# Sharing the expert sums of the context tokens among ScalarE, Pool and VectorE, and moving their end into the output merge

## The chip, the cores and the metric

The kernel runs on 1 core of one Trainium2 chip. The metric is device time in microseconds (us) of one execution. PE is the matrix engine, DVE VectorE, ACT ScalarE, POOL or Pool GpSimd, and SP the queue that issues most loads.

## The reference, cut to what matters

Two layers work on 512 latent tokens and, with a learned modulation of their own, on 128 context tokens. Each token mixes (attention, short convolution, bidirectional recurrence, merged by gates), is normalised, and then passes through a layer of experts: for each token 8 heads x 16 best keys choose 128 experts, each with a row u and a row v of 1024 numbers.

```
        ue = jnp.take(u_tab, idx, axis=0)
        ve = jnp.take(v_tab, idx, axis=0)
        act = jax.nn.gelu(jnp.einsum('td,thkd->thk', xb, ue).astype(jnp.float32), approximate=False)
        return jnp.einsum('thk,thkd->td', (g * act).astype(ve.dtype), ve)
...
    ff = peer(h, p['peer_wq'], p['peer_keys'], p['peer_u'], p['peer_v'])
    x = layer_norm(DEEPNORM_ALPHA * x + g_f * ff, p['ln_g'][1], p['ln_b'][1])
```

For the 128 context tokens, one per partition, this means 128 dot products of `h` with a gathered row u and 128 weighted sums `y += w * v`. The modulated result is the next layer's input (`h_ctx`), and the last layer's is the output `y_prompt`.

## The kernel before

A layer runs as a row of stages; all engines meet between two of them. In the order of the program: input and mixing of the context tokens (`context_in`), a scan, `context_out`, then for the latent tokens `recurrent_branch` (projection, scan, second projection with the tiles `rf_`, second scan), `recurrent_out` (`recm`), `conv_branch` (`conv_`), `attention` (projection `qkv_`, then `attention_core`, tiles `att_`), `attention_out` (the output merge, tiles `attm_`), `context_end` (tiles `ce_`), and `experts` for the latent tokens (about half of the time).

All projections are one function, `projections` (L161). A job multiplies the tokens with a 1024 x 1024 weight matrix in two halves. SP loads a matrix of 2 MB into `ring` (two buffers); ACT rounds each half to a high part, and DVE forms the low part by a subtraction (`low_part`, L152, the "split"); PE needs both. PE then fills output tiles, which ACT or DVE empties. After tile t DVE may run a number of small jobs of another party, the object `behind`: `hooks` (L178) spreads its `n_vector` jobs evenly over the tiles. Pool runs the party's `pool` or `pool_all`.

That party is the experts of the context tokens (`ContextExperts`, L2202). Pool gathers a row of u or v for all 128 tokens with one indirect DMA of 512 KB (L2307) into one of five slots of `ctx_rows`; a gather waits until the slot's last user is done. DVE makes a dot product in one instruction (L2313) or adds `w * row` to `ctx_y` in one (L2337). `DOTS = 24, 56, 48` gives the dots in the stages `rf_`, `recm` and `conv_`; `SUMS = 48, 52, 28` the sums in `conv_`, `qkv_` and `attm_`, all of them on DVE. In `rf_`, Pool also refines the gates of the recurrence (L1051, L1052, 16 pairs), and gathers stand between the pairs. Dots in `conv_` use three slots and sums two; before and after that sums use five.

In the attention core DVE works through 32 units (a head of a block of 128 tokens: a maximum L873, a difference of two softmaxes L882, a division L887), and Pool has nothing. In layer 0 that stage also computes the next layer's modulation from 12 weight loads of 2 MB (L402). In the merge, Pool works on vectors for the next part (L1128 to L1132).

`context_end` (L2963) loads six rows, forms `LN(alpha x + gate y)`, stores it, and for layer 0 modulates, transposes it on PE and copies it to `h_ctx` on ACT.

## Time and profile before

| | |
|---|---|
| median of 3 runs | 6462.62 us (6458.78 to 6463.95) |
| profiled execution | 6454.55 us, its span 6452.7 us, mean granted clock 0.949 |
| busy: PE | 5330.4 us (83%) |
| busy: DVE | 4310.9 us (67%) |
| busy: ACT | 2317.6 us (36%) |
| busy: POOL | 1969.1 us (31%) |

The span is the time from the first to the last instruction. A busy share is an average over all stages, and says little here: stages differ in what ends last in them. The rows further down are therefore cut by stage. Times in a timeline count from the span's start. "Idle before" is the engine's time without work ahead of an instruction, and behind the arrow stands what ended it. An instruction's duration includes time in which it was held by another engine.

### The profile page before, as it was taken

To read this page: it belongs to the slowest core of one execution; us is meant where nothing else is said; L and a number is where in the kernel's file an instruction comes from. 1 tells how busy PE (TensorE), PEld (TensorE's weight loads), DVE (VectorE), ACT (ScalarE), POOL (GpSimd) and SP (SyncE) were. 2 spreads that over 40 slices of the span, in tenths; PEclk is the share of its full clock that TensorE was granted. 3 is DMA by queue.
4 is the path that set the end of the run, shared out by engine and by line. 5 is a ranking of instruction groups with operands and counts; after the bars stand their busy time and mean duration, and the time that the engine had idled before them with its cause. 6 is when DMAs were issued, how large, how long until landed. Compare 5 with 4: busy or idle time off the path is not lost. (4 is left out here: it accounts for less than half of the span.)

```text
span 6452.7 us, 92227 instructions
## 1 busy us (share of the span) xinstructions
PE 5330.4 (83%) x34024; PEld 3655.2 (57%) x34024; DVE 4310.9 (67%) x8431; ACT 2317.6 (36%) x5243; POOL 1969.1 (31%) x1837
## 2 busy tenths in 40 slices
PE   7979868988868888888789798789889688888886
PEld 6758757777764333333267687677677533333332
DVE  3147767877677777777741377768787777777777
ACT  1122552222414444444412135521233244444444
POOL 0002434442114333333300024344421233333332
PEclk8989989999989999999999899899999899999999
DMA  8732226776449999999976323277743699999998
GB/s 343 311 154 81 89 78 233 281 258 228 180 157 418 421 421 421 420 418 419 416 282 233 154 81 101 77 256 272 251 142 140 231 421 421 421 421 419 415 419 342
DMA packets 296531, 1813.69 MB, mean 281 GB/s; under 512 B 35120, under 2 KB 58864, under 8 KB 141940
## 3 DMA queue, kind: packets, MB, share of 16 engines
q0 software_dynamic: 221184, 1342.28, 52.3%
q1 hardware_dynamic: 74902, 465.54, 18.9%
q8 instruction: 273, 4.47, 0.3%
q14 instruction: 172, 1.41, 0.1%
HBM read 1792.74 MB, written 17.04 MB: 280 GB/s over the span
## 5 line engine op out<-in xcount | busy, mean ns | idle before, releaser
L2093 PE MATMUL ex_ps_y<-ring,peer_small 128*128 128x512 f32 x1632 | 789.4, 611 | 201.2 <-ACT peer_small L2043 199.1
L2093 PE MATMUL ex_ps_y<-early,peer_small 128*128 128x512 f32 x1632 | 785.1, 609 | 203.4 <-ACT peer_small L2043 201.4
L1934 DVE CUSTOM_DVE_ANT_0 early<-early,ex_ps_h 128x1024 f32<-128x1024 f32 x408 | 498.0, 1220 | 299.1 <-DMA early<-in_peer_uv,ex_index 295.6
L1934 DVE CUSTOM_DVE_ANT_0 ring<-ring,ex_ps_h 128x1024 f32<-128x1024 f32 x408 | 497.8, 1220 | 286.3 <-DMA ring<-in_peer_uv,ex_index 282.6
L2035 ACT ACTIVATE ex_act<-ex_dot 128x1 f32<-128x1 f32 x1024 | 205.6, 201 | 1261.1 <-DVE ex_dot L1934 1260.0
L2307 POOL DMA_INDIRECT ctx_rows<-in_peer_uv,ctx_iv x256 | 357.6, 1397 | 921.4 <-DVE ctx_y L2337 541.1
L2093 PEld LDWEIGHTS ex_ps_y<-early,peer_small 128*128 128x128 f32 x1632 | 285.3, 191 | 622.4 <-issue 622.0
L2093 PEld LDWEIGHTS ex_ps_y<-ring,peer_small 128*128 128x128 f32 x1632 | 285.3, 191 | 622.0 <-issue 621.6
L1670 POOL DMA_INDIRECT early<-in_peer_uv,ex_index x408 | 395.1, 968 | 633.6 <-PE ex_ps_y L2093 567.1
L1670 POOL DMA_INDIRECT ring<-in_peer_uv,ex_index x408 | 388.5, 952 | 649.5 <-PE ex_ps_y L2093 593.5
L2093 PE MATMUL ex_ps_y<-ex_slot,peer_small 128*128 128x512 f32 x832 | 407.7, 617 | 114.1 <-ACT peer_small L2043 113.1
L2313 DVE CUSTOM_DVE_ANT_0 ctx_rows<-ctx_rows,ctx_h 128x1024 f32<-128x1024 f32 x256 | 318.3, 1253 | 158.5 <-DMA ctx_rows<-in_peer_uv,ctx_iu 157.9
L2043 ACT ACTIVATE peer_small<-ident,ex_w 128x128 f32<-128x128 f32 x1024 | 411.3, 402 | 33.5
L2307 POOL DMA_INDIRECT ctx_rows<-in_peer_uv,ctx_iu x256 | 329.1, 1286 | 216.3 <-DVE ctx_dots L2313 153.2
L2337 DVE SCALAR_TENSOR_TENSOR ctx_y<-ctx_rows,ctx_dots,ctx_y 128x1024 f32<-128x1024 f32 x254 | 326.9, 1287 | 60.8 <-issue 29.9
L1934 DVE CUSTOM_DVE_ANT_0 ex_slot<-ex_slot,ex_ps_h 128x1024 f32<-128x1024 f32 x208 | 253.7, 1220 | 145.0 <-DMA ex_slot<-in_peer_uv,ex_index 142.9
L1670 POOL DMA_INDIRECT ex_slot<-in_peer_uv,ex_index x208 | 198.7, 955 | 474.8 <-PE ex_ps_y L2093 316.7
L2093 PEld LDWEIGHTS ex_ps_y<-ex_slot,peer_small 128*128 128x128 f32 x832 | 147.5, 194 | 331.2 <-issue 330.9
L2039 ACT ACTIVATE ex_w<-ex_act,ex_share 128x1 f32<-128x1 f32 x1024 | 301.5, 294 | 37.4 <-ACT ex_act L2035 0.4
L2073 PE MATMUL ex_ps_q<-h_high,ex_wh 128*128 128x256 f32 x512 | 236.3, 462 | 26.6 <-DVE h_low L152 26.6
L266 PE MATMUL rf_ps<-rf_wh,h_high 128*128 128x256 f32 x768 | 219.1, 285 | 28.3 <-DVE rf_wl L152 28.3
L266 PE MATMUL conv_ps<-h_high,conv_wh 128*128 128x512 f32 x512 | 210.9, 412 | 27.0 <-DVE conv_wl L152 27.0
(556 smaller groups left out, 12955.2 us busy)
## 6 DMA issues: line engine op xcount, KB each, us to landing
ring<-in_w_in SPq DMA_DIRECT2D x75, 2048.0 KB, 9.1
ci_w<-in_w_in SPq DMA_DIRECT2D x35, 2048.0 KB, 9.8
ring<-in_w_branch SPq DMA_DIRECT2D x23, 2048.0 KB, 10.1
ring<-in_mod_w SPq DMA_DIRECT2D x22, 2048.0 KB, 8.3
room<-in_peer_wq SPq DMA_DIRECT2D x14, 1024.0 KB, 26.1
co_w<-in_w_out SPq DMA_DIRECT2D x4, 2048.0 KB, 14.7
ring<-in_peer_wq SPq DMA_DIRECT2D x4, 2048.0 KB, 13.1
co_w<-in_peer_wq SPq DMA_DIRECT2D x4, 2048.0 KB, 7.9
```

What stands on the lines that cost most here:

```text
L266: last = nc.tensor.matmul(ps[:, at:at + cols], lhs, rhs, start=k == 0 and n == 0, stop=k == KT - 1 and n == 2)
L1670: nc.gpsimd.indirect_dma_start(pair_row[slot(n, s)], None, T["peer_uv"], bass.IndirectOffsetOnAxis(ap=index[n % 4][:, s:s + 1], axis=0)).t ...
L1934: V.tensor_tensor_reduce(out=row, in0=row, in1=ps_h[:], scale=1.0, scalar=0.0, op0=ALU.mult, op1=ALU.add, accum_out=dot[n % 2][:, s:s + 1] ...
L2035: act.activation(act_v[n % 2][:, at], dot[n % 2][:, at], ACT.Gelu).then_inc(gelu_done, 1)
L2039: act.activation(wgt[n % 2][:, at], act_v[n % 2][:, at], ACT.Copy, scale=share[n % 2][:, at]).then_inc(weighed, 1)
L2043: act.activation(diag[s % DIAGS], ident[:], ACT.Copy, scale=wgt[n % 2][:, at]).then_inc(diag_ready, 1)
L2073: last = nc.tensor.matmul(ps_q[:, a, 0:width], w[h % 2][:, k, w_cols], h_split[x][:, k, toks], start=k == 0 and m == 0, stop=k == KT - 1 a ...
L2093: last = nc.tensor.matmul(ps_y[n % 2][:, c:c + 512], diag[s % DIAGS], v_row[slot(n, s)][:, c:c + 512], start=s == 0, stop=s == TOPK - 1)
L2307: self.nc.gpsimd.indirect_dma_start(self.row(s), None, self.table, bass.IndirectOffsetOnAxis(ap=index[:, j:j + 1], axis=0)).then_inc(self. ...
L2313: self.nc.vector.tensor_tensor_reduce(out=self.row(s), in0=self.row(s), in1=self.h[:], scale=1.0, scalar=0.0, op0=ALU.mult, op1=ALU.add, a ...
L2337: V.scalar_tensor_tensor(self.y[:], self.row(s), w, self.y[:], ALU.mult, ALU.add).then_inc(self.added, 1)
```

## The change

The numbers of dots become 6, 58 and 64 in `rf_`, `recm` and `conv_`. The 128 sums are spread in another way:

- `conv_`: 30 sums. ACT scales the gathered row in place by its weight, at a hook of its own after a tile, and Pool adds it to `ctx_y`. The slots are 0 and 1; dots keep slots 2 to 4.
- `qkv_`: 16 sums of the same kind (slots 3 and 4), and 45 on DVE as before (slots 0 to 2), but into `ctx_h`, which is free by then.
- attention core: 20 sums on Pool alone, a scaling and an addition each, with five slots.
- `attm_`: 17 sums on DVE, with slots 0 and 1.

The stage `context_end` goes. `ContextEnd` is the party of the merge: of its 51 hooks on DVE over 36 tiles, the first 17 are the sums (tiles 0 to 11), and hooks 23 to 36 are the steps of the end (tiles 16 to 26); ACT takes the root at a hook. SP loads three rows into slots 2 to 4 ahead of the merge's weights, and the others behind them. The transposes into `h_ctx` are done by the next layer's `context_in`, ahead of its first product.

```
                 beside.load(sp)
+                behind.load(sp)
                 for c, job in enumerate(weighted[1:], 1):
                     if c >= 2:
                         sp.wait_ge(low_done, splits(2 * (c - 2) + 1))
                     sp.dma_start(ring[c % 2][:], job.weights).then_inc(w_loaded[c % 2], 16)
+                behind.load_last(sp)
                 beside.finish(sp)
+                behind.stored(sp)
...
                             act.wait_ge(tile_done, t + 1)
                             empty(act, job, e, t, m, steps).then_inc(slot_free[t % 4], 1)
+                        for j in hooks(behind.n_scalar, t):
+                            behind.scalar(act, j)
...
+            @block.gpsimd
+            def _(pool):
+                behind.pool_all(pool)
...
-DOTS = 24, 56, 48
-SUMS = 48, 52, 28
-U_FIRST, V_FIRST = DOTS[0] + DOTS[1], SUMS[0]
-PHASES = (("u", 0, U_FIRST, (0, 1, 2, 3, 4)), ("u", U_FIRST, CHOICES - U_FIRST, (2, 3, 4)),
-          ("v", 0, V_FIRST, (0, 1)), ("v", V_FIRST, CHOICES - V_FIRST, (0, 1, 2, 3, 4)))
+DOTS = 6, 58, 64
+U_FIRST = DOTS[0] + DOTS[1]
+SUMS = {"conv": 30, "qkv_pool": 16, "qkv": 45, "att": 20, "attm": 17}
+PHASES = (("u", U_FIRST, (0, 1, 2, 3, 4)), ("u", CHOICES - U_FIRST, (2, 3, 4)), ("conv", SUMS["conv"], (0, 1)),
+          ("qkv_pool", SUMS["qkv_pool"], (3, 4)), ("qkv", SUMS["qkv"], (0, 1, 2)), ("att", SUMS["att"], (0, 1, 2, 3, 4)), ("attm", SUMS["attm"], (0, 1)))
+ON_VECTOR = SUMS["qkv"] + SUMS["attm"]
+ON_POOL = CHOICES - ON_VECTOR
...
+    def gather_v(self, pool, phase, j):
+        s, n, behind, v, done = LANDINGS[phase, j]
+        if behind is not None:
+            if phase in ("qkv", "attm"):
+                pool.wait_ge(self.added_too, self.l * ON_VECTOR + behind)
+            else:
+                pool.wait_ge(self.added, self.l * ON_POOL + behind)
+        pool.sem_inc(self.going, 1)
+        self.nc.gpsimd.indirect_dma_start(self.row(s), None, self.table, bass.IndirectOffsetOnAxis(
+            ap=self.index_v[:, v:v + 1], axis=0)).then_inc(self.landed[s], 16)
...
+    def arrived(self, eng, phase, j):
+        s, n, behind, v, done = LANDINGS[phase, j]
+        eng.wait_ge(self.weighed, 2 * self.l + v // 64 + 1)
+        eng.wait_ge(self.landed[s], 16 * (self.l * LANDED[s] + n))
+        return self.row(s), self.dots[:, v:v + 1], done
...
+    def scale(self, eng, phase, j):
+        row, w, done = self.arrived(eng, phase, j)
+        if phase == "att":
+            self.nc.gpsimd.tensor_scalar(row, row, w, None, ALU.mult).then_inc(self.scaled, 1)
+        else:
+            eng.activation(row, row, ACT.Copy, scale=w).then_inc(self.scaled, 1)
+
+    def add_on_pool(self, pool, phase, j):
+        s, n, behind, v, done = LANDINGS[phase, j]
+        P_ = self.nc.gpsimd
+        pool.wait_ge(self.scaled, self.l * ON_POOL + done + 1)
+        if done == 0:
+            P_.tensor_scalar(self.y[:], self.row(s), 1.0, None, ALU.mult).then_inc(self.added, 1)
+            return
+        pool.wait_ge(self.added, self.l * ON_POOL + done)
+        P_.tensor_tensor(self.y[:], self.y[:], self.row(s), ALU.add).then_inc(self.added, 1)
...
-            V.tensor_scalar(self.y[:], self.row(s), w, None, ALU.mult).then_inc(self.added, 1)
+        if done == 0:
...
+        dve.wait_ge(self.added_too, self.l * ON_VECTOR + done)
+        V.scalar_tensor_tensor(self.h[:], row, w, self.h[:], ALU.mult, ALU.add).then_inc(self.added_too, 1)
...
+        e, n, added = self.experts, SUMS["conv"], 0
+        e.gather_v(pool, "conv", 0)
+        e.gather_v(pool, "conv", 1)
         for j in range(DOTS[2]):
-            self.experts.gather(pool, "u", U_FIRST + j)
-            self.experts.gather(pool, "v", j)
...
+            e.gather_u(pool, U_FIRST + j)
+            while added < n and (added + 2) * DOTS[2] <= (j + 1) * n:
+                e.add_on_pool(pool, "conv", added)
+                if added + 2 < n:
+                    e.gather_v(pool, "conv", added + 2)
+                added += 1
+        for j in range(added, n):
+            e.add_on_pool(pool, "conv", j)
+            if j + 2 < n:
+                e.gather_v(pool, "conv", j + 2)
...
+        for j in range(SUMS["qkv"]):
+            e.gather_v(pool, "qkv", j)
+            while added < n and (added + 2) * SUMS["qkv"] <= (j + 1) * n:
+                e.add_on_pool(pool, "qkv_pool", added)
+                if added + 2 < n:
+                    e.gather_v(pool, "qkv_pool", added + 2)
+                added += 1
...
+        e, n = self.experts, SUMS["att"]
+        for j in range(CTX_SLOTS):
+            e.gather_v(pool, "att", j)
+        for j in range(n):
+            e.scale(pool, "att", j)
+            e.add_on_pool(pool, "att", j)
+            if j + CTX_SLOTS < n:
+                e.gather_v(pool, "att", j + CTX_SLOTS)
...
+    n_vector = n_scalar = 3 * SUMS["attm"]
+    FIRST_STEP = SUMS["attm"] + 6
...
+    def load(self, sp):
+        e = self.experts
+        sp.dma_start(self.gate, mod_row(e.T, e.l, 1, 5)).then_inc(self.first_in, 16)
+        sp.dma_start(self.x, e.T["ctx_rows"]).then_inc(self.first_in, 16)
...
+    def load_last(self, sp):
+        e = self.experts
+        sp.wait_ge(e.added_too, (e.l + 1) * ON_VECTOR)
+        sp.dma_start(self.beta, e.T["ln_b"][bass.ds(e.l, 1), 1, :].to_broadcast([P, D])).then_inc(self.last_in, 16)
+        if self.goes_on:
+            sp.dma_start(self.plus, mod_row(e.T, e.l + 1, 1, 0)).then_inc(self.last_in, 16)
+            sp.wait_ge(self.summed, self.nth)
+            sp.dma_start(self.shrink[:], mod_row(e.T, e.l + 1, 1, 1)).then_inc(self.last_in, 16)
...
+    def pool_all(self, pool):
+        for j in range(SUMS["attm"]):
+            self.experts.gather_v(pool, "attm", j)
...
+    def scalar(self, act, j):
+        if j == self.FIRST_STEP + 6:
+            act.wait_ge(self.var, self.nth)
+            act.activation(self.root[:], self.mv[:, 1:2], ACT.Sqrt).then_inc(self.rooted, 1)
...
+        e, V = self.experts, self.experts.nc.vector
+        if j < SUMS["attm"]:
+            e.add_on_vector(dve, "attm", j)
+        x, y, c = self.x, e.y[:], j - self.FIRST_STEP
...
+        if c == 0:
+            dve.wait_ge(e.added_too, (e.l + 1) * ON_VECTOR)
+            dve.wait_ge(e.added, (e.l + 1) * ON_POOL)
+            V.tensor_tensor(y, y, e.h[:], ALU.add).then_inc(self.summed, 1)
+            dve.wait_ge(self.summed, self.nth)
+        if c == 1:
+            dve.wait_ge(self.first_in, 48 * self.nth)
+            step(1, V.tensor_tensor(y, y, self.gate, ALU.mult))
+        if c == 2:
+            step(2, V.scalar_tensor_tensor(x, x, ALPHA, y, ALU.mult, ALU.add))
...
+            if c == 13:
+                V.tensor_tensor(self.h_ctx[:].rearrange("p k t -> p (k t)"), self.shrink[:], self.plus, ALU.add)
...
+                if l:
+                    for k in range(KT):
+                        last = nc.tensor.transpose(ps_att[:, k * P:(k + 1) * P], h_ctx[:, k, :], ident[:])
+                    last.then_inc(h_turned, 1)
+                    pe.wait_ge(ht_ready, 1)
...
-                    x = {"B0": by_k(o_t), "B1": by_k(o_conv)}.get(kind, h_ctx)
+                    x = {"B0": by_k(o_t), "B1": by_k(o_conv)}.get(kind, h_t)
...
-                attention(nc, l, T, h_split, by_token(rooms[0]), by_token(rooms[1]), ring, ident, Sums(E, s1, SUMS[1], True))
-                attention_out(nc, l, T, h_split, by_token(rooms[0]), by_channel(rooms[1]), main, by_token(rooms[1]), norm, rows, ring, ident, Sums(E, s2, SUMS[2]))
-                context_end(nc, l, T, h_ctx, ident, E)
+                attention(nc, l, T, h_split, by_token(rooms[0]), by_token(rooms[1]), ring, ident, SharedSums(E), PoolSums(E))
+                attention_out(nc, l, T, h_split, by_token(rooms[0]), by_channel(rooms[1]), main, by_token(rooms[1]), norm, rows, ring, ident, ContextEnd(E, context, h_ctx, endings))
```

What Pool runs in `rf_`, layer 0, at the stage's start (L1051 and L1052 are the refining pair; `ctx_iu` the list of rows u), before:

```order
L2307 DMA ctx_rows<-in_peer_uv,ctx_iu 128x1024 x2
L1051 TENSOR_TENSOR room_3<-room_3,rec_bounds_383 128x256
L1052 TENSOR_TENSOR room_3<-room_3,ctx_y 128x256
L2307 DMA ctx_rows<-in_peer_uv,ctx_iu 128x1024 x2
L1051 TENSOR_TENSOR room_3<-room_3,rec_bounds_383 128x256
L1052 TENSOR_TENSOR room_3<-room_3,ctx_y 128x256
L2307 DMA ctx_rows<-in_peer_uv,ctx_iu 128x1024 x2
L1051 TENSOR_TENSOR room_3<-room_3,rec_bounds_383 128x256
```

and now, where L1062 and L1063 are the same pair and L2337 is the gather:

```order
L1062 TENSOR_TENSOR room_3<-room_3,rec_bounds_395 128x256
L1063 TENSOR_TENSOR room_3<-room_3,ctx_y 128x256
L2337 DMA ctx_rows<-in_peer_uv,ctx_iu 128x1024
L1062 TENSOR_TENSOR room_3<-room_3,rec_bounds_395 128x256
L1063 TENSOR_TENSOR room_3<-room_3,ctx_y 128x256
L1062 TENSOR_TENSOR room_3<-room_3,rec_bounds_395 128x256
L1063 TENSOR_TENSOR room_3<-room_3,ctx_y 128x256
L2337 DMA ctx_rows<-in_peer_uv,ctx_iu 128x1024
```

Of 29 gathers there 11 are left, at most one behind a pair, and two pairs can follow each other.

Pool at the start of the attention core, layer 0, now (before, it has no row there; L2348 gathers a row v, L2377 scales it, L2389 adds it):

```order
L2348 DMA ctx_rows<-in_peer_uv,ctx_iv 128x1024 x5
L2377 TENSOR_SCALAR ctx_rows<-ctx_rows,ctx_dots 128x1024
L2389 TENSOR_TENSOR ctx_y<-ctx_y,ctx_rows 128x1024
L2348 DMA ctx_rows<-in_peer_uv,ctx_iv 128x1024
L2377 TENSOR_SCALAR ctx_rows<-ctx_rows,ctx_dots 128x1024
L2389 TENSOR_TENSOR ctx_y<-ctx_y,ctx_rows 128x1024
L2348 DMA ctx_rows<-in_peer_uv,ctx_iv 128x1024
```

The last three rows go on to the 20th sum, without a gather in the last five.

What DVE runs in the merge, layer 0, from its first sums on (L336 writes the attention's rows for the next product), before:

```order
L2337 SCALAR_TENSOR_TENSOR ctx_y<-ctx_rows,ctx_dots,ctx_y 128x1024
L152 TENSOR_TENSOR attm_wl_591<-ring_7,attm_wh_589 128x2048
L2337 SCALAR_TENSOR_TENSOR ctx_y<-ctx_rows,ctx_dots,ctx_y 128x1024 x2
L152 TENSOR_TENSOR attm_wl_592<-ring_7,attm_wh_590 128x2048
L336 SCALAR_TENSOR_TENSOR att_out_low<-attm_ps_585,attm_column,att_out_high 128x8x128
L336 SCALAR_TENSOR_TENSOR att_out_low<-attm_ps_586,attm_column,att_out_high 128x8x128
L2337 SCALAR_TENSOR_TENSOR ctx_y<-ctx_rows,ctx_dots,ctx_y 128x1024
L336 SCALAR_TENSOR_TENSOR att_out_low<-attm_ps_587,attm_column,att_out_high 128x8x128
L2337 SCALAR_TENSOR_TENSOR ctx_y<-ctx_rows,ctx_dots,ctx_y 128x1024
L336 SCALAR_TENSOR_TENSOR att_out_low<-attm_ps_588,attm_column,att_out_high 128x8x128
L2337 SCALAR_TENSOR_TENSOR ctx_y<-ctx_rows,ctx_dots,ctx_y 128x1024 x2
L152 TENSOR_TENSOR attm_wl_591<-ring_6,attm_wh_589 128x2048
```

and now, where L2398 is the sum and L343 the former L336:

```order
L2398 SCALAR_TENSOR_TENSOR ctx_h<-ctx_rows,ctx_dots,ctx_h 128x1024 x2
L152 TENSOR_TENSOR attm_wl_606<-ring_7,attm_wh_604 128x2048
L2398 SCALAR_TENSOR_TENSOR ctx_h<-ctx_rows,ctx_dots,ctx_h 128x1024 x3
L152 TENSOR_TENSOR attm_wl_607<-ring_7,attm_wh_605 128x2048
L343 SCALAR_TENSOR_TENSOR att_out_low<-attm_ps_600,attm_column,att_out_high 128x8x128
L2398 SCALAR_TENSOR_TENSOR ctx_h<-ctx_rows,ctx_dots,ctx_h 128x1024 x2
L343 SCALAR_TENSOR_TENSOR att_out_low<-attm_ps_601,attm_column,att_out_high 128x8x128
L2398 SCALAR_TENSOR_TENSOR ctx_h<-ctx_rows,ctx_dots,ctx_h 128x1024
L343 SCALAR_TENSOR_TENSOR att_out_low<-attm_ps_602,attm_column,att_out_high 128x8x128
L2398 SCALAR_TENSOR_TENSOR ctx_h<-ctx_rows,ctx_dots,ctx_h 128x1024
L343 SCALAR_TENSOR_TENSOR att_out_low<-attm_ps_603,attm_column,att_out_high 128x8x128
L2398 SCALAR_TENSOR_TENSOR ctx_h<-ctx_rows,ctx_dots,ctx_h 128x1024 x5
L152 TENSOR_TENSOR attm_wl_606<-ring_6,attm_wh_604 128x2048
```

Ahead of the next `attm_wl` of ring 0 there stood 7 sums, and now 14; the rows that they read come through two slots in place of five.

## Rows read from the trace of the kernel before

**Rows 1.** The table by stages: us of window and PE, PEld, DVE, ACT, POOL busy (count), PEclk, DMA share, GB/s.
```profile
748.00:844.00 96.00, 50.65 (x408) 49.95 (x408) 44.17 (x65) 20.59 (x36) 70.84 (x63) 0.79 0.62 200
1126.00:1390.00 264.00, 237.66 (x984) 189.10 (x984) 205.02 (x244) 50.36 (x46) 125.37 (x98) 0.95 0.76 271
1390.00:1549.70 159.70, 142.57 (x792) 122.88 (x793) 141.09 (x170) 35.29 (x39) 73.66 (x52) 0.95 0.71 248
1549.70:1715.60 165.90, 144.93 (x1521) 112.47 (x1522) 100.67 (x206) 72.45 (x161) 0.00 (x0) 0.94 0.48 172
1715.60:1876.80 161.20, 145.34 (x824) 126.41 (x824) 122.41 (x146) 35.99 (x36) 49.04 (x32) 0.95 0.54 193
1876.80:1902.40 25.60, 2.00 (x9) 1.63 (x10) 9.99 (x12) 2.56 (x4) 0.00 (x0) 0.50 0.40 143
3962.70:4060.40 97.70, 52.63 (x409) 51.94 (x409) 45.61 (x65) 20.62 (x37) 71.11 (x64) 0.77 0.61 196
4768.60:4895.10 126.50, 120.22 (x752) 94.15 (x753) 96.54 (x194) 72.42 (x161) 0.00 (x0) 0.94 0.05 18
5056.00:5075.90 19.90, 0.00 (x1) 0.03 (x1) 6.84 (x9) 1.46 (x3) 0.00 (x0) 0.50 0.37 133
```

**Rows 2.** Groups of instructions of Pool in the second recurrent projection, layer 0.
```profile
L2307 POOL DMA_INDIRECT ctx_rows<-in_peer_uv,ctx_iu x29 | 38.0, 1311 | 6.3 <-issue 4.4
```

**Rows 3.** Waits of PE in the same stretch: us in total, times, longest.
```profile
PE rf_ps L266 <- DVE rf_wl L152: 13.5, 2, 11.1
```

**Rows 4.** The timeline at that stage's end: start, us, instruction, idle before it.
```profile
837.15 0.94 POOL L2307 DMA_INDIRECT ctx_rows<-in_peer_uv,ctx_iu  x1 [0.30 <-issue]
...
844.32 0.77 PE L1283 MATMUL scan_ps_d<-scan_lfh,scan_suffix 128*128 128x512 f32 x1 [32.10 <-PEq L90]
```

**Rows 5.** The timeline in the end of the context tokens, layer 0.
```profile
1887.84 1.23 DVE L3012 TENSOR_TENSOR ctx_y<-ctx_y,ce_gate 128x1024 f32<-128x1024 f32 x1 [15.34 <-DMA ce_shrink<-mod_rows]
...
1898.23 1.97 PE L2996 MATMUL ce_ps<-ident,ctx_h 128*128 128x128 f32 x8 [29.78 <-DVE ctx_h L3026]
...
1900.24 1.02 ACT L3005 ACTIVATE h_ctx<-ce_ps 128x1024 f32<-128x1024 f32 x1 [7.78 <-PE ce_ps L2996]
```

**Rows 6.** The timelines of DVE, Pool and PE in the output merge, layer 0.
```profile
1737.70 1.28 DVE L2337 SCALAR_TENSOR_TENSOR ctx_y<-ctx_rows,ctx_dots,ctx_y 128x1024 f32<-128x1024 f32 x1
...
1739.79 2.21 POOL L2307 DMA_INDIRECT ctx_rows<-in_peer_uv,ctx_iv  x1 [15.48 <-DVE ctx_y L2337]
...
1763.87 2.29 DVE L152 TENSOR_TENSOR attm_wl<-ring,attm_wh 128x2048 fp32r<-128x2048 f32 x1 [8.10 <-ACT attm_wh L296]
...
1772.36 0.39 PE L266 MATMUL attm_ps<-att_out_high,attm_wh 128*128 128x512 f32 x1
```

**Rows 7.** DMA issues in the same merge: line, count, KB, us to landing.
```profile
ring<-in_w_branch SPq DMA_DIRECT2D x2, 2048.0 KB, 10.6
...
ctx_rows<-in_peer_uv,ctx_iv POOLq DMA_INDIRECT x28, 6.3
```

**Rows 8.** Groups of Pool over the whole span, each shape apart.
```profile
L1128 POOL TENSOR_SCALAR ring<-ring 128x1024 f32<-128x1024 f32 x2 | 6.0, 2986 | 0.1
...
L1130 POOL TENSOR_TENSOR room<-room,ring 128x1024 f32<-128x1024 f32 x2 | 4.8, 2395 | 0.2
...
L1377 POOL TENSOR_SCALAR room<-room 128x512 f32<-128x512 f32 x28 | 17.4, 621 | 2.3
```

**Rows 9.** The timeline of the same merge, where DVE and Pool meet.
```profile
1860.49 2.06 DVE L2337 SCALAR_TENSOR_TENSOR ctx_y<-ctx_rows,ctx_dots,ctx_y 128x1024 f32<-128x1024 f32 x1
...
1861.55 3.27 POOL L1131 TENSOR_TENSOR ring<-ring,room 128x1024 f32<-128x1024 f32 x1
```

**Rows 10.** A group of DVE in the attention core, layer 1.
```profile
L882 DVE SCALAR_TENSOR_TENSOR att_p<-att_p,att_ratio 128x640 f32<-128x640 f32 x32 | 28.3, 884 | 1.1
```

**Rows 11.** Waits of PE in the attention core, layer 0.
```profile
PE att_ps_mod L402 <- DMA ring<-in_mod_w: 14.7, 11, 3.0
```

**Rows 12.** Waits of PE in the convolution, layer 0.
```profile
PE conv_ps L266 <- DVE conv_wl L152: 14.8, 10, 3.7
```

More of the change, by code:

```diff
@@ L2427, in pool_all @@
     def pool_all(self, pool):
[L2428 to L2429 removed]
+        e, n, added = self.experts, SUMS["qkv_pool"], 0
+        e.gather_v(pool, "qkv_pool", 0)
+        e.gather_v(pool, "qkv_pool", 1)
+        for j in range(SUMS["qkv"]):
[5 more added lines that the diff above has]
+                added += 1
```

207 lines of the change are left out of this document (104 added, 103 removed).

## The prediction

> **What bounds the kernel now.** I read the table by stages first [rows 1]. Its columns are busy time of PE, weight loads, DVE, ACT and Pool, the granted clock and the DMA share. PE fills most stages (237.66 of 264.00 us in the convolution, 142.57 of 159.70 in the query, key and value projection), so most work of the context tokens lies beside PE and costs nothing by itself. Three stretches are different. In the second recurrent projection PE works 50.65 of 96.00 us and Pool 70.84. In the end of the context tokens PE works 2.00 of 25.60 us in layer 0 and nothing in layer 1: pure serial time. In the attention core Pool does nothing at all.
>
> Next I read who is last in those stretches. In the recurrent projection Pool runs 29 gathers of 1.31 us and 16 refining pairs [rows 2]; PE waits 13.5 us there for a split of weights, once for 11.1 [rows 3], because the split stands on DVE behind dots whose rows are not there yet. PE then stands idle 32.10 us until the next stage, which starts 6.2 us after Pool's last gather ended [rows 4]. So Pool sets that stage's end. In the end of the context tokens DVE first waits 15.34 us for rows from DMA, and the last ACT copy starts at 1900.24 [rows 5].
>
> **The change, part by part** (per layer; the sum is made against the profiled run's 6454.55 us).
>
> *Dots leave the recurrent projection.* 18 of 29 gathers go, 18 x (1.31 + 0.30 issue gap) = 29 us of Pool, and the dots that held the split. PE ended at 844.32 - 32.10 = 812.2; without the 11.1 us wait 801.1; then one refining pair (2: Pool's 70.84 less the gathers' 38.0, by 16) and a stage change of 5 (6.2 here, with gathers in flight to the end) give 808 in place of 844.3: **-36**. Bounds: -22 if PE's end does not move, -40 if the other 2 us of its waits go too. Layer 1's stage is 97.70 us with the same busy times: -36 again. Together -72. Two more dots in the next stage: +1.
>
> *The end's stage disappears.* Its 25.60 us (layer 0) and 19.90 us (layer 1, no transposes) go: **-45.5**. The stage change before it stays, as that of the merge. Eight transposes and one copy, 1.97 and 1.02 us [rows 5], move to the head of layer 1's context input, on its path: +3. ScalarE's root and DVE's 14 steps run between later tiles of the merge, where fewer sums stand than before (17 for 28), so I cost them at nothing; without that cover they are the 9.99 us of DVE in that stage [rows 1].
>
> *The merge.* Sums fall from 28 to 17, but they lie in the first 12 of 36 tiles, on two slots instead of five. Before, DVE reached its first sum 22 us into the stage, finished the split for the product's first half at 1766.16, and PE needed it at 1772.36 [rows 6]; 6 us of slack. Now 14 sums stand ahead of that split. Two rows are there at once. Each slot then turns in: sum's end to gather 0.8 (1738.98 to 1739.79), landing 6.3 (median of 28) [rows 7], the sum 1.28, so about 8.4 us for two sums. From 1737.7 that is 12 sums x 4.2 = 50, plus the first two and the split: 1737.7 + 2.6 + 50 + 2.3 = 1793, as other work fits into the waits; against 1772.4 that is +21, and PE has little reserve later (145.34 busy of 161.20). I take +21. The tail of sums after PE's end goes, -4. **+17** each layer, +34. Bounds: 0, the split just in time, with landings near 3, which the median speaks against; +45 if each row took as long as a weights load of the same stretch, 10.6 [rows 7].
>
> *The attention core.* 20 times scale, add, gather on Pool. The add: 2.40 us alone (L1130, the same form) [rows 8]. The scale has two neighbours: 2.99 us for one operation on 128x1024 (L1128) and 0.62 us for multiply and add on 128x512 (L1377), 1.24 for this size [rows 8]. I take 2.99, since it has one operation too. With a gather of 1.3 and gaps, 7 us each, 140 in all, behind a first landing of 6. Layer 0's core lasts 165.90 and waits on weights for the modulation, 14.7 us of PE's waits [rows 11]: it covers them but for 4 us of stage change (one that Pool gathers in ends that much later) and some lost turns of DVE: +8. Layer 1's lasts 126.50: 6 + 140 + 5 = 151, **+24**. Bounds of the two: +8 (1.24 us scales) to +50 (DVE blocked as below).
>
> *Whether Pool and DVE block each other.* Where a Pool add and a DVE sum met, the sum took 2.06 us for 1.28 and the next Pool add 3.27 for 2.40 [rows 9]; each ends when the other's end allows it. So adds cost 2.40 to 3.3 of Pool, and DVE loses up to 2.4 at a meeting. The core's L882 (0.88 us, 32 times) [rows 10] reads two SBUF tiles and will meet Pool nearly every unit; at 1 us each that is 32 us on layer 1's chain, beside the 24 already taken, not on top of it.
> The Trainium skill, page "SBUF — State Buffer", section "Who interferes with whom", says that a VectorE instruction with two SBUF inputs contends with a GpSimd instruction that reads SBUF, and that the shared ports are an exclusive lock; by that rule the change would lose more than I take, as in the slower rival. The trace agrees with 2.06 for 1.28 us.
>
> *The convolution.* DVE loses 48 sums of 1.28 [rows 6] and gains 16 dots, each about as long: -41 us of 205. PE's waits on splits are 14.8 us [rows 12], so -12 at best. Pool now has 94 gathers and 30 adds: 94 x (1.28 + 0.30) + 30 x 3.3 = 248 us, where 1.28 is 125.37 / 98 [rows 1]. There are about 252 us before the stage change. Pool is full, its order is fixed, and each add waits for ScalarE's scale (1.02 us for a copy of that size [rows 5]; ScalarE is 19% busy), so gathers behind it come late and dots hold DVE. I take **+8** each, bounds -12 and +35.
>
> *The projection.* DVE (141.09 of 159.70) loses 7 sums, -9 us, and meets 16 adds, 16 x 1.3 = +20. Pool: 61 x (1.42 + 0.30) + 16 x 3.3 = 158 us for 155. **+8** each, bounds -5 and +30.
>
> Sum: -72 - 45.5 + 34 + 32 + 16 + 16 + 5 = **-14.5**, so 6440 for a run like the profiled one. The median of the runs shown, 6462.62, stands 8 above that run: 6448.
>
> The page "GPSIMD Engine Reference" of the Trainium skill, section "4.1 Engine selection", calls one-input work on GpSimd roughly line-rate; the 2.99 us of L1128 speak against it and the 0.62 of L1377 for it. By it the core of layer 1 would cost +8 and the sum would be -30.
>
> **The rivals.** About 0.2% (13 us) is what a measurement of this kernel can tell from no change.
>
> A, my forecast: gains of 117 and new costs of 103 nearly cancel. Own range 6420 to 6480.
>
> B, Pool is cheaper than I think: scales at 1.24, adds meet DVE seldom, and the lighter DVE in the convolution gives PE its waits back. Core +4 and +6, convolution -12 each, projection 0: -117.5 + 34 + 10 - 24 + 5 = -92.5, 6370. For it: the row L1377, DVE's 41 us. Against: L1128, and Pool full in the convolution.
>
> C, slower: Pool becomes the bound of the convolution and of the projection, because gathers and adds wait for DVE's splits and DVE for adds. It decides from a mean gather of 1.33 us in the convolution (94 g + 28 + 99 = 252) and 1.37 in the projection (61 g + 18 + 53 = 155); today's means are 1.28 and 1.42 with no adds beside them, so it is close. At 1.6 the convolution's Pool needs 277, +25, the projection's +14, and DVE's lost turns make that +20; core +12 and +35: -117.5 + 34 + 50 + 40 + 47 + 5 = +58.5, 6521.
>
> D, the change doesn't free the recurrent projection: its end is then set by ScalarE and PE (clock 0.79 there), with -20 for -72. Sum +37, 6500. Against: PE idle 32.10 us while Pool gathers.
>
> **How the numbers follow.** A 0.42: of it faster 0.23, same 0.17, slower 0.02. B 0.25, faster. C 0.23, slower. D 0.10: same 0.04, slower 0.06. So faster 0.48, same 0.21, slower 0.31. The likeliest is A's 6448. The range runs from inside B (6385, which leaves out some 0.12) to just past C's 6521 (6530, leaving out some 0.08).
>
> **What would show it.** The recurrent projection at 60 us with PE idle a few us at its end; no stretch after the merge where PE stands; in the merge PE waiting about 20 us on a split of weights, with DVE waiting for gathered rows; Pool busy to the end of layer 1's core, which then lasts 150; Pool at over 90% in the convolution with that stage at 265 to 275. I am wrong if Pool's scales are near 1.2 us, if the merge's split comes in time, or if the convolution moves by over 15 us.

## The result, and the profile after

The changed kernel takes 6563.12 us (median; 6550.26 to 6570.24), the kernel before 6463.28 in the same runs: ratio 1.0158, 95% interval 1.0146 to 1.0171, so 100 us slower. The range ended at 6530. The profiled execution has a span of 6567.6 us, 114.9 above the 6452.7 of before. One of the four executions of the last version below was slow (7962.45 us at a granted clock of 0.61) and is left out of the time given for it.

The table by stages of the changed kernel, columns as in [rows 1]: the second recurrent projection, the convolution, the projection, the core and the merge of layer 0, then the recurrent projection, the core and the merge (with the end in it) of layer 1.

```profile
747.40:813.00 65.60, 48.35 (x409) 48.06 (x409) 21.11 (x29) 20.50 (x37) 45.76 (x46) 0.90 0.48 148
1095.00:1396.90 301.90, 241.91 (x985) 191.13 (x986) 203.56 (x228) 83.07 (x77) 201.08 (x126) 0.92 0.67 233
1396.90:1598.90 202.00, 154.22 (x792) 131.65 (x793) 160.99 (x163) 52.99 (x55) 122.72 (x77) 0.88 0.65 219
1598.90:1774.20 175.30, 145.98 (x1521) 112.28 (x1522) 122.55 (x206) 72.48 (x161) 125.31 (x60) 0.94 0.61 222
1774.20:1947.80 173.60, 146.30 (x825) 126.09 (x825) 121.14 (x148) 37.47 (x38) 33.11 (x21) 0.93 0.47 167
4010.20:4076.60 66.40, 49.88 (x408) 49.58 (x408) 20.92 (x29) 20.62 (x36) 45.78 (x45) 0.87 0.46 146
4862.40:5010.40 148.00, 120.97 (x752) 93.25 (x753) 112.07 (x194) 72.44 (x161) 125.48 (x60) 0.90 0.26 86
5010.40:5190.40 180.00, 152.20 (x824) 131.72 (x824) 120.01 (x145) 37.54 (x37) 32.87 (x21) 0.91 0.44 155
```

Against [rows 1]: the recurrent projection 65.60 for 96.00; the convolution 301.90 for 264.00; the projection 202.00 for 159.70; the core 175.30 for 165.90 and, in layer 1, 148.00 for 126.50; merge and end together 173.60 for 186.80, and 180.00 for 180.80. Layer 1's convolution (302.1, before 266.9) and projection (202.0, before 162.7) repeat layer 0's. So two gains of 62 and 14 us stand against 31 in the core, 73 in the convolution and 82 in the projection; the last 5 are spread over the other stages.

What engine is the convolution waiting for? The waits of DVE, and under them the longest of PE, in that stage (us in total, times, longest):

```profile
DVE ctx_rows L2354 <- DMA ctx_rows<-in_peer_uv,ctx_iu: 90.3, 22, 9.7
...
DVE conv_wl L152 <- ACT conv_wh L299: 7.1, 2, 6.0
...
PE conv_ps L269 <- DVE conv_wl L152: 44.3, 13, 8.3
```

DVE is busy for 203.56 us and waits for 90.3 + 7.1: together 301 of 301.90. The busy time and the waits of any engine fill a stage; what tells is whom it waits for. DVE waits for gathered rows and for ACT, never for PE. PE waits for DVE: its 44.3 us are waits for splits that stand in DVE's order behind dots whose rows have not landed. And Pool waits for DVE, as a piece of the timeline shows (DVE, Pool):

```profile
1142.29 1.23 DVE L2354 CUSTOM_DVE_ANT_0 ctx_rows<-ctx_rows,ctx_h 128x1024 f32<-128x1024 f32 x1 [9.71 <-DMA ctx_rows<-in_peer_uv,ctx_iu]
...
1144.32 1.16 POOL L2337 DMA_INDIRECT ctx_rows<-in_peer_uv,ctx_iu  x1 [5.37 <-issue]
```

DVE stands 9.71 us for a row and makes the dot, and 0.80 us after its end Pool, idle for 5.37 us, issues the next dot's gather. The profile mostly names no releaser for such waits of Pool, but 14 of them, 53.5 us together, end 0.80 us after a dot. So the ring of DVE's dots and Pool's gathers sets this stage, not PE. Seen from PE, the 38 us are 29.5 more of waits for splits, 4.4 more at the change to the next stage, and 4.3 of its own busy time, at a granted clock of 0.92 for 0.95. The view of DVE's waits in the kernel before:

```profile
DVE ctx_rows L2313 <- DMA ctx_rows<-in_peer_uv,ctx_iu: 31.0, 10, 6.9
DVE ctx_y L2337 <- issue: 13.3, 12, 2.6
DVE conv_wl L152 <- ACT conv_wh L296: 6.9, 2, 5.8
DVE ctx_y L2337 <- DMA ctx_rows<-in_peer_uv,ctx_iv: 5.6, 2, 4.6
```

There it was 205.02 + 31.0 + 13.3 + 6.9 + 5.6 = 262 of 264.00. DVE did not wait for PE before either; PE's 237.66 us hid that. The waits for rows went from 37 to 90 us (all of DVE's waits from 57 to 97), and DVE's busy time stayed at 204 although 41 us of work had left it.

In the projection, the waits of DVE in the changed kernel:

```profile
DVE ctx_h L2398 <- DMA ctx_rows<-in_peer_uv,ctx_iv: 22.9, 12, 4.7
DVE ctx_h L2395 <- DMA ctx_rows<-in_peer_uv,ctx_iv: 8.9, 1, 8.9
DVE qkv_wl L152 <- ACT qkv_wh L299: 6.2, 2, 5.0
DVE att_lam_pr L672 <- DMA att_lam_in<-in_lam: 2.8, 1, 2.8
```

160.99 busy and 41 of waits make 202. Here, too, DVE's busy time rose (141.09 before) with 7 sums fewer.

Where DVE's extra time comes from is seen in the timeline of the convolution: DVE, Pool, DVE.

```profile
1224.96 2.90 DVE L625 CAST conv_out_high<-room 128x512 fp32r<-128x512 f32 x1
...
1225.14 2.42 POOL L2389 TENSOR_TENSOR ctx_y<-ctx_y,ctx_rows 128x1024 f32<-128x1024 f32 x1
...
1231.51 0.43 DVE L625 CAST conv_out_high<-room 128x512 fp32r<-128x512 f32 x1
```

The same cast takes 0.43 us alone and 2.90 when it meets a Pool add of 2.42: it ends 0.3 us after the add does.

### The profile page after: what moved, and what is told of

Same layout as the page of the kernel before. It is cut to its first block and busy times, and to the rows that moved or that the text cites. A ratio compares the mean times of both kernels' runs of the same rounds, so it can differ in the third digit from the quotient of the medians.

```text
span 6567.6 us, 92427 instructions
## 1 busy us (share of the span) xinstructions
PE 5368.1 (82%) x34024; PEld 3679.4 (56%) x34024; DVE 4322.1 (66%) x8301; ACT 2422.2 (37%) x5335; POOL 2399.3 (37%) x2009
## 5 line engine op out<-in xcount | busy, mean ns | idle before, releaser
L2354 DVE CUSTOM_DVE_ANT_0 ctx_rows<-ctx_rows,ctx_h 128x1024 f32<-128x1024 f32 x256 | 332.7, 1319 | 261.3 <-DMA ctx_rows<-in_peer_uv,ctx_iu 260.7
L2348 POOL DMA_INDIRECT ctx_rows<-in_peer_uv,ctx_iv x256 | 325.9, 1273 | 395.1 <-DVE ctx_h L2398 189.4
L2337 POOL DMA_INDIRECT ctx_rows<-in_peer_uv,ctx_iu x256 | 335.1, 1309 | 310.8 <-DVE ctx_dots L2354 184.4
L1681 POOL DMA_INDIRECT ex_slot<-in_peer_uv,ex_index x208 | 198.7, 955 | 471.8 <-PE ex_ps_y L2104 321.4
L2389 POOL TENSOR_TENSOR ctx_y<-ctx_y,ctx_rows 128x1024 f32<-128x1024 f32 x130 | 325.9, 2507 | 5.6
L2379 ACT ACTIVATE ctx_rows<-ctx_rows,ctx_dots 128x1024 f32<-128x1024 f32 x92 | 106.0, 1152 | 522.0 <-DMA ctx_rows<-in_peer_uv,ctx_iv 522.0
```

What stands on the lines that cost most here:

```text
L1681: nc.gpsimd.indirect_dma_start(pair_row[slot(n, s)], None, T["peer_uv"], bass.IndirectOffsetOnAxis(ap=index[n % 4][:, s:s + 1], axis=0)).t ...
L2337: self.nc.gpsimd.indirect_dma_start(self.row(s), None, self.table, bass.IndirectOffsetOnAxis(ap=self.index_u[:, j:j + 1], axis=0)).then_in ...
L2348: self.nc.gpsimd.indirect_dma_start(self.row(s), None, self.table, bass.IndirectOffsetOnAxis(ap=self.index_v[:, v:v + 1], axis=0)).then_in ...
L2354: self.nc.vector.tensor_tensor_reduce(out=self.row(s), in0=self.row(s), in1=self.h[:], scale=1.0, scalar=0.0, op0=ALU.mult, op1=ALU.add, a ...
L2389: P_.tensor_tensor(self.y[:], self.y[:], self.row(s), ALU.add).then_inc(self.added, 1)
```

## The experiments

Stage times are given for layer 0 and layer 1, read from the first PE instruction of a stage to that of the next. In the changed kernel the convolution is 301.9 and 302.1, the projection 202.0 and 202.0. Each experiment ran once, up to the versions that beat both kernels. In the runs whose edit leaves them alone, the convolution lasts 296.9 to 302.3 us and the projection 198.7 to 202.5; smaller differences tell nothing. The expectations weigh three theories: 'ports' (a Pool add holds DVE's operations), 'queue' (adds stand ahead of gathers in Pool's order) and 'scale' (ACT, waiting to scale a row, is late for the rest).

### Adds of 8 columns

```
-        P_.tensor_tensor(self.y[:], self.y[:], self.row(s), ALU.add).then_inc(self.added, 1)
+        if phase == "att":
...
+        P_.tensor_tensor(self.y[:, 0:8], self.y[:, 0:8], self.row(s)[:, 0:8], ALU.add).then_inc(self.added, 1)
```

In the convolution and the projection the rest of each such sum is left out.

> Pool's 46 adds a layer in the convolution and the projection work on 8 of 1024 columns; the rest of these sums is left out. Order, waits and gathers stay. In the changed kernel the convolution lasts 302 us (264 before) and the projection 202 (160 before). Theory 'ports': a Pool add holds what DVE needs for its second operand or its fast mode, DVE loses the time of the add, and PE waits for DVE's splits. Theory 'queue': adds stand ahead of gathers in Pool's order, so rows come late, and DVE stands at dots and sums whose rows have not landed. Both expect a large fall here: convolution under 275, projection under 175. Theory 'scale': ACT stands at its scaling until the gathered row has landed, and the rounding of weights behind it is late. It expects no large change: over 290 and over 192.

Measured 6451 us (the kernel before 6450 on that chip): convolution 261.8 and 261.8, projection 184.4 and 182.4. Stages of layer 0 (convolution, projection):

```profile
1090.10:1351.90 261.80, 235.20 (x984) 187.63 (x984) 167.10 (x228) 83.08 (x76) 141.11 (x126) 0.96 0.75 269
1351.90:1536.40 184.50, 149.47 (x794) 128.05 (x794) 132.22 (x164) 52.75 (x55) 91.38 (x77) 0.91 0.71 240
```

In the convolution the loss is gone without the adds' width, although DVE still waits 86.0 us there for dots' rows. In the projection 18 of 42 us are gone; DVE's busy time there fell by 29, yet its waits for rows grew (from 32 to 43 us), and 20 to 25 us more than before remain. The bound "under 175" was missed.

### Fills that read nothing

```
-        P_.tensor_tensor(self.y[:], self.y[:], self.row(s), ALU.add).then_inc(self.added, 1)
+        if phase == "att":
...
+        P_.memset(self.row(s), 0.0)
+        P_.memset(self.y[:], 0.0).then_inc(self.added, 1)
```

The sums of the convolution and the projection are left out.

> The same adds are replaced by two fills of 128x1024 on Pool, some 2 us together, which write and read nothing; these sums are left out. Pool's queue is held nearly as long as by the add (2.4 to 2.6 us), but no operand is read. 'Ports' (by reading): convolution under 275 and projection under 175, with DVE's times of single operations back at those of the kernel before. 'Queue': convolution 285 to 300, projection 190 to 200. 'Scale': unchanged, 302 and 202.

Measured 6502 us: convolution 273.1 and 282.7, projection 193.6 and 192.2. The two stages of layer 0, and DVE's wait for dots' rows in the first:

```profile
1095.80:1368.90 273.10, 240.24 (x985) 191.30 (x985) 172.50 (x228) 82.78 (x77) 178.23 (x155) 0.94 0.73 258
...
1368.90:1562.50 193.60, 150.66 (x792) 128.83 (x793) 132.40 (x163) 52.94 (x55) 111.64 (x93) 0.90 0.67 229
...
DVE ctx_rows L2354 <- DMA ctx_rows<-in_peer_uv,ctx_iu: 92.1, 25, 10.2
```

Two fills held Pool for 1.94 us, where an add held it for 2.63. DVE's busy time in the convolution fell from 203.56 to 172.50, 31 us for 29 adds (the first of the 30 sums is a copy), while its waits for rows stayed (92.1 for 90.3). The stage fell by 29 us in layer 0 and by 19 in layer 1. Most of that is put down to the operands that an add reads; but Pool was also busy for 23 us less, and the run doesn't part the two. The rest, down to 262, comes with the fills themselves: Pool's time, and DVE's casts, two of which a pair of fills still held for 2.3 us. In the projection DVE's busy time fell by the same 29 us, but only 8 and 10 came out: its waits for rows grew from 32 to 52 us. Neither theory is right alone; 'queue' gave about the projection's size, 'ports' the convolution's in layer 0.

### No scaling on ACT

```
-        pool.wait_ge(self.scaled, self.l * ON_POOL + done + 1)
+        if phase == "att":
...
+            self.arrived(pool, phase, j)
...
-    n_vector, n_scalar = DOTS[2], SUMS["conv"]
+    n_vector, n_scalar = DOTS[2], 0
...
-    n_vector, n_scalar = SUMS["qkv"], SUMS["qkv_pool"]
+    n_vector, n_scalar = SUMS["qkv"], 0
```

The multiplication by the weight is left out.

> ACT does not scale the 46 rows, Pool waits for the landed row itself and adds it without its weight; the multiplication by the weight is left out there. 'Scale': convolution under 280, projection under 180. 'Ports' and 'queue': 295 to 305 and 195 to 205, since the adds stay as they are.

Measured 6568 us: 299.4 and 297.0, 201.3 and 200.9, all within what these stages vary by. ACT stands for landing rows for 187 us in the convolution of the changed kernel, and it costs nothing that can be seen. 'Scale' falls.

### The old dots with the new sums

```
-DOTS = 6, 58, 64
+DOTS = 24, 56, 48
```

> Dots go back to 24, 56 and 48; the sums stay as in the changed kernel. The second recurrent projection goes back from 66 to 96 us in both layers. In the convolution 48 dots use the three slots in place of 64. 'Queue': a slot's turn is some 14 us there (64 turns in three slots make 300), so 48 would need 225, and the stage falls to under 275. 'Ports': 30 adds block DVE as before, and DVE has 16 dots, 20 us, less: 280 to 300. The projection stays at 202 in both.

Measured 6534 us: recurrent projection 96.5 and 99.0, convolution 253.0 and 251.3, projection 200.9 and 198.7. The convolution, and DVE's waits in it:

```profile
1131.80:1384.80 253.00, 231.92 (x984) 185.95 (x984) 193.05 (x196) 83.25 (x76) 183.34 (x110) 0.97 0.70 245
...
DVE ctx_rows L2354 <- DMA ctx_rows<-in_peer_uv,ctx_iu: 45.5, 14, 9.8
```

With 48 dots the same 30 adds by ACT and Pool make the convolution 11 to 16 us faster than before the change: under 275, as 'queue' expected, not the 280 to 300 of 'ports'. Sixteen more dots cost 50: the waits for rows in the three slots go from 45.5 to 90.3, and DVE is busy for 10 us more. With short adds 64 dots took 262 us. So the loss needs both parts, the 64 dots through three slots and the full adds; no run gave the dots of this stage more slots.

### The projection without Pool's sums, with three and with five slots

```
-SUMS = {"conv": 30, "qkv_pool": 16, "qkv": 45, "att": 20, "attm": 17}
+SUMS = {"conv": 30, "qkv": 45, "att": 20, "attm": 17}
...
-          ("qkv_pool", SUMS["qkv_pool"], (3, 4)), ("qkv", SUMS["qkv"], (0, 1, 2)), ("att", SUMS["att"], (0, 1, 2, 3, 4)), ("attm", SUMS["attm"], (0, 1)))
+          ("qkv", SUMS["qkv"], (0, 1, 2)), ("att", SUMS["att"], (0, 1, 2, 3, 4)), ("attm", SUMS["attm"], (0, 1)))
```

The 16 sums are left out. In the second run the slots of `qkv` are `(0, 1, 2, 3, 4)`.

> The projection keeps its 45 sums on DVE with three slots; the 16 sums of ACT and Pool there are left out. With adds of 8 columns the stage was 183 us, 23 above the kernel before, though nothing of weight was left on Pool. 'Slots' (45 sums through three slots, each turn a gather, a landing of 5 to 6 us and a sum, behind other gathers): stays at 170 to 185. 'Scaling' (ACT's stand at the landings delays its tiles): 160 or less.

> As the run with three slots, 16 sums left out, but the 45 sums use all five slots. 'Slots': 150 to 158, below the 160 of the kernel before, which had 52 sums. 'Scaling': the same as with three slots.

Measured 169.1 and 171.7 with three slots, 149.5 and 149.8 with five (6500 and 6442 us in all). The stage with three, then with five, each with DVE's wait for rows:

```profile
1394.20:1563.30 169.10, 145.66 (x794) 125.93 (x794) 132.38 (x164) 35.21 (x39) 63.31 (x45) 0.91 0.63 213
...
DVE ctx_h L2398 <- DMA ctx_rows<-in_peer_uv,ctx_iv: 23.5, 19, 3.3
```

```profile
1389.80:1539.30 149.50, 140.31 (x794) 122.23 (x794) 131.60 (x164) 35.29 (x39) 65.78 (x45) 0.96 0.69 240
...
DVE ctx_h L2398 <- DMA ctx_rows<-in_peer_uv,ctx_iv: 3.5, 3, 2.3
```

DVE's busy time is the same 132, and 20 us of length are the slots. 'Slots' holds. So, taken in this order, the projection's +42 is 33 for the 16 sums of ACT and Pool and 20 for three slots, less 10 that 52 sums cost over 45.

### The core with a quicker scaling, and the merge with five slots

```
-          ("qkv_pool", SUMS["qkv_pool"], (3, 4)), ("qkv", SUMS["qkv"], (0, 1, 2)), ("att", SUMS["att"], (0, 1, 2, 3, 4)), ("attm", SUMS["attm"], (0, 1)))
+          ("qkv_pool", SUMS["qkv_pool"], (3, 4)), ("qkv", SUMS["qkv"], (0, 1, 2)), ("att", SUMS["att"], (0, 1, 2, 3, 4)), ("attm", SUMS["attm"], (0, 1, 2, 3, 4)))
...
-            self.nc.gpsimd.tensor_scalar(row, row, w, None, ALU.mult).then_inc(self.scaled, 1)
+            self.nc.gpsimd.tensor_scalar(row, row, w, 0.0, ALU.mult, ALU.add).then_inc(self.scaled, 1)
...
```

The three loads of `load` move into `load_last`, the 17 sums are spread over the first 20 hooks, and the steps begin at hook 22.

> Two edits of the changed kernel that lie in different stages. In the attention core Pool's scaling is written with two operations (multiply, then add zero). In the merge the 17 sums use five slots, and the three first rows of the end are loaded behind the last sum. Core, layer 1 (148 us, Pool busy 125): if Pool's chain ends it and two operations run at the 0.62 us for 512 columns seen elsewhere, a scaling is 1.25 in place of 2.89, Pool falls to 93 and the stage to 127 to 132; if the number of operations makes no difference, 148 stays. Merge (174 and 180 us): if the two slots hold the split behind 14 sums, it falls by 15 to 20, to 155 to 165; the rival, that it is the end's steps on DVE that lengthen it, expects no change.

Measured 6539 us. Merge 165.2 and 166.8, from 173.6 and 180.0, where 155 to 165 was expected. DVE's wait for rows in layer 0's merge fell from 26.6 to 2.3 us, so the two slots did hold it; how much of the 8 and 13 us is theirs and how much comes from the later loads and the other spread, the run doesn't part. Core: 177.7, and 158.0 in layer 1, ten us *longer* than 148, where 127 to 132 was expected. Groups of Pool and of DVE in layer 1's core:

```profile
L2377 POOL TENSOR_SCALAR ctx_rows<-ctx_rows,ctx_dots 128x1024 f32<-128x1024 f32 x20 | 23.7, 1185 | 2.9 <-DMA ctx_rows<-in_peer_uv,ctx_iv 2.5
...
L893 DVE SCALAR_TENSOR_TENSOR att_p<-att_p,att_ratio 128x640 f32<-128x640 f32 x32 | 61.2, 1914 | 1.1
```

The scaling is 1.19 us for 2.89, as the two-operation row had it, and still the core grew. The timeline of the same stretch shows why (Pool, DVE, Pool, DVE):

```profile
4900.97 2.34 POOL L2389 TENSOR_TENSOR ctx_y<-ctx_y,ctx_rows 128x1024 f32<-128x1024 f32 x1
...
4900.94 3.06 DVE L893 SCALAR_TENSOR_TENSOR att_p<-att_p,att_ratio 128x640 f32<-128x640 f32 x1
...
4906.36 2.34 POOL L2389 TENSOR_TENSOR ctx_y<-ctx_y,ctx_rows 128x1024 f32<-128x1024 f32 x1
...
4906.33 3.06 DVE L893 SCALAR_TENSOR_TENSOR att_p<-att_p,att_ratio 128x640 f32<-128x640 f32 x1
```

Pool's add and DVE's L893 start 0.03 us apart, and 5.39 us later again. L893, held to 3.06 us for 0.88, ends 0.7 us after the add; the unit is as long as Pool's turn, and so the two stay in step for as long as Pool has sums. With the slow scaling Pool's turn was 7.2 us, and L893 kept its 0.88.

### The same core with fills for its adds

```
-            self.nc.gpsimd.tensor_scalar(row, row, w, None, ALU.mult).then_inc(self.scaled, 1)
+            self.nc.gpsimd.tensor_scalar(row, row, w, 0.0, ALU.mult, ALU.add).then_inc(self.scaled, 1)
...
+        if phase == "att":
+            P_.memset(self.row(s), 0.0)
+            P_.memset(self.y[:], 0.0).then_inc(self.added, 1)
+            return
```

The sums of the core are left out.

> The core's scaling with two operations, as in the run where layer 1's core rose to 158 us though Pool's work there fell to 93. Now its 20 adds are replaced by two fills that read nothing, some 2 us together; these sums are left out. 'In step': DVE's L893 reads two tiles and falls behind the same add in each unit (3.06 us for 0.88), so its units run at Pool's period of 5.4 us; without a read in the add the core falls to 127 to 135 with L893 at 0.9. 'Gathers': what slows DVE is Pool's gathers or its scaling; the core stays over 145.

Measured 135.1 us in layer 1 (6570 in all: its convolution and projection are those of the changed kernel). L893 of DVE there:

```profile
L893 DVE SCALAR_TENSOR_TENSOR att_p<-att_p,att_ratio 128x640 f32<-128x640 f32 x32 | 33.2, 1036 | 1.1
```

The add's reading was what held the units: L893's mean fell from 1.91 us to 1.04, with two fills of 1.90 us together in the place of an add of 2.42. 135.1 lies at the upper end of what 'in step' gave.

### Versions that beat both kernels

All keep the merge with five slots and put 52 sums of the projection on DVE with five slots. First, 74 dots ahead of the convolution:

```
-DOTS = 6, 58, 64
-SUMS = {"conv": 30, "qkv_pool": 16, "qkv": 45, "att": 20, "attm": 17}
+DOTS = 6, 74, 48
+SUMS = {"conv": 30, "qkv": 52, "att": 20, "attm": 26}
```

> Dots 6, 74 and 48 (the convolution keeps 48, and the stage before it takes the 18 that leave the second recurrent projection). Sums: 30 in the convolution by ACT and Pool, 52 on DVE with five slots in the projection, 20 on Pool in the core with the scaling of two operations, 26 on DVE with five slots in the merge, the end's steps behind them. By stages against the kernel before, both layers: recurrent projection -62, convolution -25, projection 0, core +8 and +4, merge and end -20 and -15, the stage that takes 18 dots 0 to +20: 6345 to 6385 us, if each effect is separate. If the gathers crowd each other again, over 6400.

Measured 6428.36 us, ratio to the kernel before 0.9951 (0.9935 to 0.9968), where 6345 to 6385 was expected. Convolution 251.2 and 252.6; but 74 dots cost the stage ahead of it 17 and 18 us, and the core with the quick scaling 14 and 31. Then, with the scaling of one operation and the merge's end steps three tiles later, against that version:

```
-DOTS = 6, 74, 48
-SUMS = {"conv": 30, "qkv": 52, "att": 20, "attm": 26}
+DOTS = 10, 66, 52
+SUMS = {"conv": 32, "qkv": 52, "att": 18, "attm": 26}
```

> As the run that was faster than the kernel before, with: dots 10, 66 and 52; 32 sums by ACT and Pool in the convolution, 52 on DVE in the projection, 18 on Pool in the core with the scaling of one operation again, 26 on DVE in the merge, whose end steps begin three tiles later so that their rows have landed. Against that run (6428): core -5 and -15, the stage with 66 dots -8 each, convolution +6 each, recurrent projection +5 each, merge -5 each: 6405 to 6425. If 10 dots bring Pool back as the bound of the recurrent projection, or 52 dots crowd the convolution, 6430 to 6450.

Measured 6413.84 us, 0.9934 (0.9917 to 0.9950): recurrent projection 72.3 and 72.6, convolution 269.2 and 268.5, where 258 was hoped for. The same with `DOTS = 6, 66, 56`:

> The same with dots 6, 66 and 56. If dots in the convolution cost what 48 and 64 gave (252 and 302 us, 3 us for each), it is 12 longer per layer than with 52 and the recurrent projection 5 shorter: 10 to 20 us slower than the run with 10, 66 and 52. If the first of them are free there, 5 to 10 faster.

Measured 6408.44 us, 0.9925 (0.9908 to 0.9941), convolution 276.5 and 280.3. The intervals of these two versions overlap, so neither is shown to be the faster: 4 dots more in the convolution cost 7 to 12 us, and 4 fewer in the recurrent projection give 6. The last, against this version:

```
-DOTS = 6, 66, 56
-SUMS = {"conv": 32, "qkv": 52, "att": 18, "attm": 26}
+DOTS = 10, 70, 48
+SUMS = {"conv": 30, "qkv": 52, "att": 18, "attm": 28}
```

> As the run with dots 6, 66 and 56 (6408, convolution 277 to 280 us), but dots 10, 70 and 48, 30 sums in the convolution and 28 in the merge. By the runs so far: convolution 252 (48 dots) for 278, recurrent projection 72 for 66, the stage with 70 dots 176 for 169, merge +2: 11 us less per layer, 6380 to 6395. If the dots that leave the convolution cost as much in the stage ahead of it, 6400 to 6415.

Measured 6392.85 us (6389.14 to 6399.53), 0.9902 (0.9881 to 0.9923), the lowest, and 2.5% below the changed kernel by the two ratios. Four of its stages: recurrent projection, the one with 70 dots, convolution, and layer 1's core.

```profile
742.30:815.80 73.50, 50.41 (x409) 49.72 (x409) 27.90 (x37) 20.60 (x37) 53.21 (x50) 0.87 0.52 161
931.50:1103.40 171.90, 148.12 (x825) 128.24 (x826) 138.16 (x213) 42.86 (x53) 86.16 (x67) 0.93 0.77 272
1103.40:1353.60 250.20, 231.46 (x984) 184.96 (x984) 189.47 (x196) 83.46 (x76) 182.55 (x110) 0.97 0.71 248
4712.20:4850.90 138.70, 124.28 (x753) 96.15 (x754) 118.54 (x194) 72.46 (x161) 112.68 (x54) 0.93 0.26 84
```

Against the kernel before, by stage over both layers: recurrent projection -45, convolution -27, merge and end -26, the stage with 70 dots +16, core +23, projection +4: -55, as the spans have it (6397.7 and 6452.7).

## Why the prediction was wrong

Between -14.5, the forecast sum, and +114.9, the profiled runs, lie 129 us. 123 of them are in two terms: the convolution and the projection, +8 a layer each, which came out four to five times as large.

*The dots leave the recurrent projection: right, smaller.* -36 was forecast, -30.7 and -31.3 came. PE's wait of 11.1 us is gone. The step that was too short is the one behind PE's end: I put one refining pair there. The end of Pool's work, and PE's wait there:

```profile
807.34 0.98 POOL L2337 DMA_INDIRECT ctx_rows<-in_peer_uv,ctx_iu  x1
...
PE scan_ps_d L1294 <- PEq L90: 17.2, 1, 17.2
```

PE ends 17.2 us ahead of the next stage, at 795.8, and Pool then still has five pairs and four gathers, the last of which ends 4.7 us ahead of that stage. Pool sets this end still.

*The end and the merge: right.* -45.5 and +34 were forecast, -11.5 in sum; it is -13.2 and -0.8, so -14. The reason was the forecast one, sums that wait for rows ahead of what PE needs. In the timeline of DVE in the merge, and PE's waits there:

```profile
1822.13 1.28 DVE L2398 SCALAR_TENSOR_TENSOR ctx_h<-ctx_rows,ctx_dots,ctx_h 128x1024 f32<-128x1024 f32 x1 [6.71 <-DMA ctx_rows<-in_peer_uv,ctx_iv]
...
1844.12 1.28 DVE L2398 SCALAR_TENSOR_TENSOR ctx_h<-ctx_rows,ctx_dots,ctx_h 128x1024 f32<-128x1024 f32 x1 [1.27 <-DMA ctx_rows<-in_peer_uv,ctx_iv]
...
1845.32 2.28 DVE L152 TENSOR_TENSOR attm_wl<-ring,attm_wh 128x2048 fp32r<-128x2048 f32 x1
...
PE attm_ps L269 <- DVE att_out_low L343: 14.9, 2, 13.1
...
PE attm_ps L269 <- DVE attm_wl L152: 5.9, 1, 5.9
```

The split of the first half of the product starts at 1845.32, right behind a sum that waited for its row, 71 us into the stage (48 before): 23 us later, where the forecast had 27. PE's two waits make 20.8 us, where 21 was forecast; but only 5.9 of them are for the split. 14.9 (4.7 before) are for L343, which stands in DVE's order behind the same late sums, and which the forecast didn't name.

*The core: right.* +8 and +24 were forecast, +9.4 and +21.5 came. Pool's groups in layer 1's core, then the end of its chain with PE's wait behind it, and last PE's wait for DVE and Pool's idle time at the end in layer 0:

```profile
L2377 POOL TENSOR_SCALAR ctx_rows<-ctx_rows,ctx_dots 128x1024 f32<-128x1024 f32 x20 | 57.8, 2891 | 3.0 <-DMA ctx_rows<-in_peer_uv,ctx_iv 2.4
L2389 POOL TENSOR_TENSOR ctx_y<-ctx_y,ctx_rows 128x1024 f32<-128x1024 f32 x20 | 47.7, 2387 | 1.7
```

```profile
5004.26 2.34 POOL L2389 TENSOR_TENSOR ctx_y<-ctx_y,ctx_rows 128x1024 f32<-128x1024 f32 x1
...
PE attm_ps L158 <- PEq L90: 20.9, 1, 20.9
...
PE att_ps_t L825 <- DVE att_p L893: 4.7, 7, 1.0
...
1774.86 1.05 POOL L2348 DMA_INDIRECT ctx_rows<-in_peer_uv,ctx_iv  x1 [30.32 <-POOLq L90]
```

In layer 1 Pool's last add ends at 5006.6, and PE has stood for 20.9 us when the merge begins. In layer 0 Pool is done 30 us before the merge begins, covered as forecast: 4.7 of the 9.4 us are PE's waits for turns that DVE lost, and 2.1 the stage change (forecast 4). Scaling 2.89 and add 2.39 are what [rows 8] gave. My lower bound for it, +8 with a scaling of 1.24, was wrong: that scaling is slower here, by the step with L893. The remark on L893 (L882 before) in the part on blocking was the right mechanism; it only decides when Pool's turn is near the unit's. With the slow scaling Pool held L892, the operation before it, instead (a mean of 0.73 us for 0.22).

*The convolution: the step that failed.* +8 with bounds of -12 and +35; it was +38 and +35. I asked whether Pool's work fits (248 of 252 us) and took PE for the bound, with DVE 41 us lighter. The runs show that PE waits for DVE, and that Pool was not full: it worked for 201 us of 302 and stood 53.5 us for dots to free a slot. Two terms were missing. The slots: I worked out a slot's turn for the merge, but not for 64 dots through three slots. In 302 us they have 14 us a turn, where the gather (1.29), the landing (5.9), the dot (1.42) and the 0.8 us to the next gather make some 9; the rest is what stands ahead in Pool's and DVE's order. The waits for rows went with the number of dots: 45.5 us with 48, 86.0 with 64 and short adds, 90.3 with 64 and full ones, and with 48 dots the stage is faster than before. And the ports: the adds took 31 us from DVE, where I took nothing for DVE beyond the general remark. Most of DVE's 41 us of relief went to that.

*The projection: failed in the same way.* +8 with bounds of -5 and +30; it was +42 and +39. Ports were priced at 20 us of DVE and cost 29, but with the fills only 8 and 10 us of length came back. What was left out is again the slots, 45 sums through three (20 us), and Pool's order, in which 16 gathers and adds stand among the gathers that DVE waits for. The first sum shows it: its row is the third in Pool's queue, behind two of Pool's own, and DVE waits 8.9 us for it (L2395). With short adds and with fills this wait is the same 8.9; without the 16 sums there is none.

*The rivals.* C named Pool as the next bound, from a mean gather of 1.33 us in the convolution. The gathers took 1.29 and 1.28 there, and Pool was busy for 201 of 302 us; the sign was C's, the mechanism was not, and the result lies beyond its 6521. What it said of DVE losing turns was right, in part. B fell with the scaling of 2.89 us and with adds that held DVE often, D with the 62 us that the recurrent projection gave. The rule of the page "SBUF — State Buffer" of the Trainium skill, section "Who interferes with whom", by which the change would lose more, is borne out: fills that read nothing gave DVE its 31 us back. Its list of what can contend names casts and one-input operations too, as the 2.90 us cast shows, and a cast that meets two fills takes 2.3 us as well.

What stays open: how the 24 us of the projection, between 193 and 169, divide between Pool's time and its 16 gathers; and what more slots would give the convolution's 64 dots.

## What to carry to other kernels

Before calling the busiest engine the bound, look at whom each engine waits for: here PE looked busy at 90%, but it waited for DVE's splits, and DVE waited for gathered rows and not for PE. Work out the turn of a ring of buffers (gather, landing, use, and the queue ahead of the gather) for every stage whose count or slots change, not only for the one that looks narrow. Work moved from VectorE to Pool is not free of VectorE: here each Pool add of 128x1024 cost VectorE 1.1 us in the convolution and 1.8 in the projection. And beware of two loops of like period that fall into step.

## What the runs showed of the hardware that was not expected

- A multiplication by a scalar on Pool, 128x1024, took 2.89 us with one operation and 1.19 with a second that adds zero.
- A quicker operation on Pool made the stage longer, from 148.0 to 158.0 us, since Pool's turn then came into step with DVE's unit.
- A Pool add held DVE's cast (0.43 to 2.90 us) as it held operations with two tiles. Two Pool fills of 0.95 us each left L893, which reads two tiles, at a mean of 1.04 for 1.91; but they held a cast for 2.3 us.
